# Two transformer blocks on one core: 32-block turns on VectorE, every row of V on TensorE, scores on 128 rows

## The reference

```python
# layer 0, first network: gated delta rule, 16 heads, both directions, chunk by chunk
a = eye + where(strict, kk * decay * beta[:, None], 0)
sol = triangular_solve(a, rhs, lower=True, unit_diagonal=True)
...
S = S * exp(g_last) + (k * exp(g_last - g)).T @ v_new
# after the mixer of both layers: 8 heads, 16 of 16384 experts per head and token
act = gelu(einsum('pd,phkd->phk', x, u_tab[idx]))
out = einsum('phk,phkd->pd', gate * act, v_tab[idx])
# layer 1: attention, 8 query heads and 2 key heads, keys normed by head, rope on the latent ones
# second network, layer 0: 8 heads of 64, causal, with a decay of its own per head
s = q @ k.T * scale + c_q[:, None] - c_k[None, :]
# second network, after each feed-forward part
x = x + sigmoid(rms_norm(x) @ w_gate) * (p @ w_proj)
```

## Time and profile before

| | |
|---|---|
| three timed runs | 4899.77 us median (4894.84 to 4905.21) |
| the profiled execution's own time | 4927.06 us |
| its span in the profile | 4925.3 us |
| PE / DVE / POOL / ACT busy | 80% / 55% / 45% / 19% |
| mean granted clock of PE | 0.894 |

### The profile page before, as it was taken

How to read it: one execution, slowest core, us unless ns; L and a number is a source line. 1 busy time by engine, 2 the same in 40 slices (tenths; PEclk the granted TensorE clock), 3 DMA queues, 4 the chain that set the end, 5 groups by cost and what they waited for, 6 DMA issues and landing times.

```text
span 4925.3 us, 42426 instructions
## 1 busy us (share of the span) xinstructions
PE 3919.4 (80%) x14663; PEld 2246.6 (46%) x14663; DVE 2713.6 (55%) x5536; ACT 931.8 (19%) x2167; POOL 2220.1 (45%) x1993
## 2 busy tenths in 40 slices
PE   6799999999967886776777778666667798875898
PEld 1459874598643332222222234433222356632584
DVE  1355653557446766666666634676665245729241
ACT  0234321333211211111111112111111111010100
POOL 1014420244117778777777750478777400008000
PEclk7699999999988988999888988888799879986899
DMA  9310002100149999999999971799999614330343
GB/s 372 113 52 1 1 27 77 43 1 1 43 159 360 380 349 347 375 379 368 394 383 372 387 273 52 257 380 361 355 373 375 248 63 129 124 117 1 105 152 122
DMA packets 380100, 1043.21 MB, mean 212 GB/s; under 512 B 31682, under 2 KB 115884, under 8 KB 379888
## 3 DMA queue, kind: packets, MB, share of 16 engines
q0 software_dynamic: 225424, 816.31, 44.3%
q1 hardware_dynamic: 154464, 224.18, 13.5%
HBM read 1039.29 MB, written 1.08 MB: 211 GB/s over the span
## 4 chain that ended last, share of the span: by engine, by line
PE 48%; POOL 15%; DMA 15%; DVE 12%; issue 7%; ACT 2%; DVEq 0%; POOLq 0%; ACTq 0%; SPq 0%
PE psum L261 12%; DMA arena<-in_peer_u,arena 9%; PE psum L1523 9%; POOL arena L1630 7%; POOL arena L1620 6%; DMA arena<-in_peer_v,arena 4%; PE psum L299 4%; PE psum L212 3%; PE psum L1041 3%; PE psum L717 3%; PE psum L1031 3%; PE psum L756 2%; DMA arena<-in_ada_w 2%; DVE arena L1690 2%; PE psum L1480 1%
## 5 line engine op out<-in xcount | busy, mean ns | idle before, releaser
L1523 PE MATMUL psum<-arena 128*128 128x512 f32 x2816 | 1438.8, 657 | 633.8 <-ACT arena L1562 335.7
L1690 DVE SCALAR_TENSOR_TENSOR arena<-arena 128x1024 bf16<-128x1024 f32 x768 | 938.9, 1225 | 704.5 <-DMA arena<-in_peer_u,arena 703.5
L1523 PEld LDWEIGHTS psum<-arena 128*128 128x128 f32 x2816 | 557.9, 209 | 1478.5 <-issue 1033.7
L1630 POOL DMA_INDIRECT arena<-in_peer_v,arena x768 | 886.9, 1155 | 248.1 <-issue 168.3
L1620 POOL DMA_INDIRECT arena<-in_peer_u,arena x768 | 848.5, 1105 | 298.8 <-issue 192.4
L261 PE MATMUL psum<-ring,arena 128*128 128x512 f32 (+2 forms) x1408 | 597.0, 588 | 27.2 <-DVE arena L2556 9.1
L261 PEld LDWEIGHTS psum<-ring,arena 128*128 128x128 f32 x1408 | 270.9, 200 | 349.1 <-issue 325.5
L212 PE MATMUL psum<-consts,arena 128*128 128x128 f32 (+1 forms) x1473 | 223.2, 300 | 171.1 <-DVE arena L362 84.5
L1140 POOL TENSOR_TENSOR arena<-arena 128x512 f32<-128x512 f32 x224 | 254.0, 1158 | 191.9 <-PE psum L1031 129.6
L299 PE MATMUL psum<-arena,ring 128*128 128x256 f32 x1408 | 312.7, 384 | 9.1 <-DVE arena L2551 7.7
L212 PEld LDWEIGHTS psum<-consts,arena 128*128 128x128 f32 (+1 forms) x1473 | 186.2, 155 | 237.4 <-issue 132.8
(11 more groups left out here) (380 smaller groups left out, 4042.0 us busy)
## 6 DMA issues: line engine op xcount, KB each, us to landing
arena<-in_ada_w SPq DMA_DIRECT2D x48, 1024.0 KB, 14.4
ring<-in_ffn_w_up SPq DMA_DIRECT2D x44, 1024.0 KB, 5.1
ring<-in_dn_w_in SPq DMA_DIRECT2D x24, 1024.0 KB, 5.3
ring<-in_peer_w_query SPq DMA_DIRECT2D x22, 1024.0 KB, 8.2
ring<-in_ffn_w_down SPq DMA_DIRECT2D x20, 1024.0 KB, 5.1
arena<-in_peer_u,arena POOLq DMA_INDIRECT x768, 6.3
arena<-in_peer_v,arena POOLq DMA_INDIRECT x768, 6.3
ring<-in_ev_w_in SPq DMA_DIRECT2D x10, 1024.0 KB, 5.2
```

Source lines behind the costliest of these rows:

```text
L1523: m = e.matmul(k.banks[4 + t % 2 * 2 + nh], self.diag[self.place[g] % self.ND], self.vsl[g % self.NV][:, nh * 512:(nh + 1) * 512], start=u ...
L1630: e.indirect_dma_start(self.vsl[g % self.NV], None, self.tables()[1], bass.IndirectOffsetOnAxis(ap=self.eid[u % 6][:, s:s + 1], axis=0)).t ...
L1690: e.scalar_tensor_tensor(self.junk[g % 2], self.us[g % self.NU], 1.0, self.h[:, u // 8, :], MUL, MUL, accum_out=self.a[u % 2][:, s:s + 1]) ...
```

## The change

In the delta rule the level-0 mask goes into T's buffer, T0 is made there in place, and a DVE transpose of 32x32 blocks makes P0 from it. The same DVE instruction makes T from P at levels 1 to 4; PE and ACT do that at level 5 only. In `Peer` the accumulator and the DVE's own slots are gone, and PE adds all 16 slots. In attention the four key tiles are normed and roped before q's transposes are awaited, with buffers of their own, and ACT takes their roots as each key tile is copied. In the even mixer q is copied by POOL into two buffers of 128 rows in which the other head's 64 rows are zero, and the decay's 8 rows stand in 128 with zeros. In `Ple` the load of p is issued by the stage before, and p is transposed and projected before the norm.

```diff
@@ delta rule, pe_chain
-                e.wait_ge(*G.at(key("lev0", ch)))
-                e.wait_ge(*V.at(key("Dk", ch)))
-                for h in range(4):
-                    m = self.turn(e, b0[:, h * 128:(h + 1) * 128], self.bufs[ch][0][:, h, :])
-                m.then_inc(*P.up(key("lev0", ch)))
...
-                    if l > 1:
-                        e.wait_ge(*S.at(key(f"T{l - 1}", ch)))
+                    if l == 6:
+                        e.wait_ge(*S.at(key("T5", ch)))
...
+                    if l < 6:
+                        e.wait_ge(*V.at(key(f"T{l - 1}", ch)))
...
-                if l < 6:
+                if l == 5:
@@ delta rule, pool_chain
-                    gL, D = self.bufs[ch][0], self.bufs[ch][1]
+                    gL, D = self.bufs[ch][3 if l == 0 else 0], self.bufs[ch][1]
@@ delta rule, dve_chain
+    def dve_turn(self, e, ch, src, dst):
+
+        a, b = (self.bufs[ch][n].rearrange("p h n -> p (h n)") for n in (src, dst))
+        return e.transpose(b, a)
...
-                e.tensor_tensor(T, rep(ident), gL, SUB).then_inc(*V.up(key("T0", ch)))
-                e.wait_ge(*P.at(key("lev0", ch)))
-                e.tensor_tensor(Pm, rep(ident), v4(self.two(ch)[0]), SUB).then_inc(*V.up(key("P0", ch)))
+                e.tensor_tensor(T, rep(ident), T, SUB).then_inc(*V.up(key("T0", ch)))
+                e.wait_ge(*V.now())
+                self.dve_turn(e, ch, 3, 4).then_inc(*V.up(key("P0", ch)))
...
                     e.tensor_tensor(Pm, Pm, v4(self.two(ch)[1]), SUB).then_inc(*V.up(key(f"P{l}", ch)))
+                    if l < 5:
+                        e.wait_ge(*V.now())
+                        self.dve_turn(e, ch, 4, 3).then_inc(*V.up(key(f"T{l}", ch)))
@@ Peer
-    OWN = (2, 6, 10, 14)
...
-            e.wait_ge(*(self.V.at(("own", old)) if self.own(old) else self.P.at(("y", old))))
+            e.wait_ge(*self.P.at(("y", g - self.NV)))
...
-                if s and u and self.own(16 * (u - 1) + s - 1):
-                    self.dve_own(e, u - 1, s - 1)
@@ attention, dve
+        for t in range(4):
+            x = self.kk[:, t, :].rearrange("p (h d) -> p h d", h=2)
+            e.wait_ge(*S.at(("k", t)))
+            e.wait_ge(*V.now())
+            norm_rows(e, V, S, x, 2, 128, self.gk.unsqueeze(1).to_broadcast([128, 2, 128]),
+                      self.sq[:, 0:256].rearrange("p (h d) -> p h d", h=2), self.stk[:, 2 * t:2 * t + 2], ("k", t))
...
         self.qt.dve(e)
@@ even mixer
+        for n in range(2):
+            e.memset(self.qz[n], 0.0).then_inc(*self.G.up())
+        e.memset(self.cz, 0.0).then_inc(*self.G.up("zero"))
+        e.memset(self.sel, 0.0).then_inc(*self.G.up())
...
+        for n in range(2):
+            rows = slice(64 * n, 64 * n + 64)
+            e.tensor_copy(self.qz[n][rows], self.qT[rows]).then_inc(*self.G.up("qz"))
...
-            e.matmul(b[:, 0:nk], self.qT[r0:r0 + 64, h // 2, t * 128:(t + 1) * 128], self.kT[r0:r0 + 64, h // 2, 0:nk],
-                     start=True, stop=False)
-            e.matmul(b[:, 0:nk], self.sel[0:8, h, :], self.cT[0:8, 0:nk], start=False, stop=True).then_inc(*P.up(("s", n)))
+            e.matmul(b[:, 0:nk], self.qz[h % 2][:, h // 2, t * 128:(t + 1) * 128], self.kT[:, h // 2, 0:nk], start=True, stop=False)
+            e.matmul(b[:, 0:nk], self.sel[:, h, :], self.cz[:, 0:nk], start=False, stop=True).then_inc(*P.up(("s", n)))
@@ Ple, pe
+        e.wait_ge(*self.lt.at("p"))
+        for t in range(2):
+            for c in range(2):
+                m = self.turn(e, self.k.banks[4][:, (2 * c + t) * 128:(2 * c + t + 1) * 128], self.p[:, t, c * 128:(c + 1) * 128])
+        m.then_inc(*self.P.up("pt"))
+        e.wait_ge(*self.V.at("pT"))
+        self.pp.pe(e)
         self.norm.pe(e)
...
-        self.pp.pe(e)
         self.gp.pe(e)
```

More of the change, by code:

```diff
@@ L1103, in act_chain @@
                     e.activation(self.bufs[ch][5], b0, ACT.Copy, bias=0.0, scale=1.0).then_inc(*S.up(key(f"X{l}", ch)))
-                if l < 6:
+                if l == 5:
                     for ch in self.chains:
                         b0 = self.two(ch)[0].rearrange("p (h n) -> p h n", h=4)
-                        e.wait_ge(*P.at(key(f"T{l}", ch)))
-                        e.activation(self.bufs[ch][3], b0, ACT.Copy, bias=0.0, scale=1.0).then_inc(*S.up(key(f"T{l}", ch)))
+                        e.wait_ge(*P.at(key("T5", ch)))
+                        e.activation(self.bufs[ch][3], b0, ACT.Copy, bias=0.0, scale=1.0).then_inc(*S.up(key("T5", ch)))
             for ch in self.chains:
@@ L1131, in pool_chain @@
                 for ch in self.chains:
-                    gL, D = self.bufs[ch][0], self.bufs[ch][1]
+                    gL, D = self.bufs[ch][3 if l == 0 else 0], self.bufs[ch][1]
                     if l == 0:
                         e.wait_ge(*V.at(key("Dk", ch)))
-                    elif l == 1:
-                        e.wait_ge(*P.at(key("lev0", ch)))
-                        e.wait_ge(*V.at(key("T0", ch)))
-                    else:
+                    elif l > 1:
                         e.wait_ge(*P.at(key(f"X{l - 1}", ch)))
@@ L1392, in __init__ @@
         self.l_v = [k.lane(f"v{n}_{name}_landed") for n in range(self.NV)]
-        self.pe_slots = [g for g in range(16 * self.units) if not self.own(g)]
-        self.place = {g: n for n, g in enumerate(self.pe_slots)}
-    def own(self, g):
-        return g < 128 and g % 16 in self.OWN
     def sc_mark(self, u):
@@ L1518, in pe_sum @@
             g = 16 * u + s
-            if not self.own(g):
-                e.wait_ge(*S.at(("dg", g)))
-                e.wait_ge(*self.l_v[g % self.NV].at(g))
-                for nh in range(2):
-                    m = e.matmul(k.banks[4 + t % 2 * 2 + nh], self.diag[self.place[g] % self.ND],
-                                 self.vsl[g % self.NV][:, nh * 512:(nh + 1) * 512], start=u % 8 == 0 and s == 0,
-                                 stop=u % 8 == 7 and s == 15)
-                m.then_inc(*P.up(("y", g)))
+            e.wait_ge(*S.at(("dg", g)))
+            e.wait_ge(*self.l_v[g % self.NV].at(g))
+            for nh in range(2):
+                m = e.matmul(k.banks[4 + t % 2 * 2 + nh], self.diag[g % self.ND], self.vsl[g % self.NV][:, nh * 512:(nh + 1) * 512],
+                             start=u % 8 == 0 and s == 0, stop=u % 8 == 7 and s == 15)
+            m.then_inc(*P.up(("y", g)))
             if s in steps:
@@ L1557, in act @@
                 g = 16 * u + s
-                if not self.own(g):
-                    n = self.place[g]
-                    if n >= self.ND:
-                        e.wait_ge(*P.at(("y", self.pe_slots[n - self.ND])))
-                    e.activation(self.diag[n % self.ND], k.const("ident"), ACT.Copy, bias=0.0,
-                                 scale=self.cf[u % 2][:, s:s + 1]).then_inc(*S.up(("dg", g)))
+                if g >= self.ND:
+                    e.wait_ge(*P.at(("y", g - self.ND)))
+                e.activation(self.diag[g % self.ND], k.const("ident"), ACT.Copy, bias=0.0,
+                             scale=self.cf[u % 2][:, s:s + 1]).then_inc(*S.up(("dg", g)))
                 if s - 3 in steps:
@@ L1669, in dve @@
         self.dve_add(e, self.nt - 1)
-    def dve_own(self, e, u, s):
-        V, g = self.V, 16 * u + s
-        c, v = self.cf[u % 2][:, s:s + 1], self.vsl[g % self.NV]
-        e.wait_ge(*self.l_v[g % self.NV].at(g))
-        e.wait_ge(*V.at(("cf", u)))
-        if u == 0 and s == self.OWN[0]:
-            e.tensor_scalar(self.acc, v, c, None, MUL).then_inc(*V.up(("own", g)))
-        else:
-            e.wait_ge(*V.at("own"))
-            e.scalar_tensor_tensor(self.acc, v, c, self.acc, MUL, ADD).then_inc(*V.up(("own", g)))
-        V.mark("own")
     def dve_dot(self, e, u, s):
@@ L1880, in __init__ @@
         self.gq, self.gk, self.cs = k.al(128), k.al(128), k.al(256)
-        self.st = k.al(8)
+        self.st, self.stk = k.al(8), k.al(8)
         self.sq = k.al(1024)
         self.tmp = [k.al(512) for _ in range(4)]
-        self.rots = [k.al(1024) for _ in range(2)]
+        self.rots, self.krots = [k.al(1024) for _ in range(2)], [k.al(256) for _ in range(2)]
         self.qT, self.kT = k.al2(8, 256), k.al2(2, 512)
@@ L1891, in __init__ @@
                                     for t in range(2)])
-        self.kt = [Turn(self, f"kT{t}", [(self.kk[:, t, :] if t < 2 else self.rots[t - 2][:, 0:256],
+        self.kt = [Turn(self, f"kT{t}", [(self.kk[:, t, :] if t < 2 else self.krots[t - 2],
                                          self.kT[:, :, t * 128:(t + 1) * 128], [lambda t=t: V.at(("k", t))])],
@@ L1959, in act @@
             e.activation(self.v[:, t, :], b[:, 256:512], ACT.Copy, bias=0.0, scale=1.0).then_inc(*S.up(("v", t)))
+            root_rows(e, self.V, S, self.stk[:, 2 * t:2 * t + 2], ("k", t))
         self.qt.act(e)
-        for t in range(4):
-            root_rows(e, self.V, S, self.st[:, 0:2], ("k", t))
         self.at.act(e)
@@ L2078, in __init__ @@
```

(7 more changed lines are left out.)

58 lines of the change are left out of this document (21 added, 37 removed).

## The result

The changed kernel takes 4759.57 us (median of 4 runs, 4734.30 to 4777.75) beside 4901.16 for the kernel before (4894.84 to 4905.21): a ratio of 0.9722, 95% interval 0.9698 to 0.9746, or 142 us. The forecast was 119 us less, and 4781. The profiled execution took 4734.30 us, the fastest of its four and 25 us under their median, where the profile of before was 26 us over the median of its four.

What follows compares the result with a forecast made beforehand. Stages run one after another, each with its own bound: PE's chain in the delta rule, neither PE nor DVE full in peer. Terms -48 - 39 - 12 - 16 - 4 = -119, from 4899.8 to 4781 us; range 4745 to 4868.

Steps and rivals of the forecast that it cites:

- A: Delta rule: DVE transposes of 0.70 us relieve PE's chain, which stays the bound narrowly; -48 us.
- step-through: Delta rule half followed by each engine's order, with waits for POOL: 345.0 us before, 320.7 after.
- signs of being wrong: DVE busy without rest in the levels, transposes of two lengths, or POOL waiting for PE; no size given.
- B: Peer stages: DVE's 32 operations a stage go to PE and POOL's issues shorten; `peer_a` -15, `peer_m` -24, together -39 us.
- C: Attention: key norms and ropes move into DVE's idle time, scores at about 3024; -12 us, -10 to -14.
- D: Even scores: matmuls on 128 rows are shorter and the clock may go to 1.00; -16 us, -7 to -22.
- fallback of -7 at half clock: Even scores: if the clock stays at half, only shorter matmuls gain, -7 us, 4790; chance inside the forecast's 0.60.
- E: Both Ple: 6.9 us leave L261's chain, but the norm's transposes come 5.0 later; -4 us, +4 to -10.
- Slow transposes: Delta rule rival: a DVE transpose takes 1.225 us and DVE bounds the level; +37 us there, 4866; chance 0.12.
- transposes that wait for POOL: Delta rule rival: DVE transposes wait for POOL as L1213 does; +31 us there, 4860; chance 0.12.
- PE as the bound of the peer stages: Rival: PE bounds both first tiles, waits behind L1480 eat gains; -12 us for the peer stages, 4808; chance 0.09.
- Half clock to the end of the even scores: Even scores rival: the clock stays at half, -7 us there, 4790; chance inside the forecast's 0.60.

Runs made afterwards that it cites:

- e4_turn_twice: Changed kernel with each DVE transpose of levels 1 to 4 made twice; 4936.65 us on another chip, delta stage 1275.4 us against 1190.1.
- e7_rhs_late: Changed kernel with three chains' right-hand side made after level 5 and the last's after level 4; ratio 0.9781 to the kernel before, 4830.2 us.
- e11: Changed kernel with the even scores' q and k product on 64 rows again, the decay's still on 128; even mixer 183.4 us against 167.5.
- e12: Changed kernel with the even scores' decay product on 8 rows again, q and k on 128; even mixer 185.6 us against 167.5.
- e5: The changed kernel itself once more, on the second chip, against the kernel before; ratio 0.9805, 93 us between the medians.
- e9: Changed kernel plus an unread two-SBUF-input DVE operation at each of 32 places per peer stage's first tile; 4816.78 us, ratio 0.9812 to the kernel before.
- e10: Changed kernel plus an unread one-input DVE sum over 128x1024 at each of the same 32 places per peer stage; 4777.19 us, ratio 0.9745 to the kernel before.
- e1: The kernel before with the delta rule's edits only; ratio 0.9908 to the kernel before on the same chip, -46 us.
- e8: Changed kernel with eight V buffers, late right-hand side, and Ple's norm transposes behind half of p's projection; 4815.02 us, ratio 0.9753 to the kernel before.

## Why the prediction was right, point by point

**A, the delta rule: -48 forecast, -51.6.** The transpose was taken as 0.70 us from the nearest one-input row and takes 0.712. What went otherwise is the sentence that PE stays the bound, narrowly. DVE was worked out as 6.6 us a level with both right-hand operations at 0.69; they take 1.1 to 1.5 each, and in the three later steps of a half the level is DVE's, 7.9 to 8.3 us. The step-through had the wait for POOL in it, and so the total was right where the sentence was not; `e4_turn_twice` shows DVE as the bound, and `e7_rhs_late` that these operations are the cause, 13.2 us where the step-through gave 12. Two of the forecast's own signs of being wrong showed: DVE busy without rest in the levels, and POOL waiting for PE. The later steps came out at 81 to 84 us against 87 to 90, inside the 80 to 86 that was said, the first at 76 against 84. The right total rests on the step-through, and that one is borne out.

The Trainium skill (SBUF — State Buffer, § Who interferes with whom) has two SBUF inputs as one condition under which a DVE instruction contends with a GpSimd instruction that reads SBUF. The trace agrees: 1227 ns for L1234 against 690, and 711 to 715 for every transpose.

**B, the peer stages: -39 forecast, -51 in the first comparison.** `peer_a` came as worked out (-15, measured -16), but by luck, from two larger terms that cancel: issues shorter by 39 us, not 21, and waits for PE of 23 us (256 x 0.09), not 6. The 21 was the issues under L1680 alone, and they are 20.7 us in the table above; nearly all of the rest are the issues under dot products, 19 us less (43.5 to 24.3), which the working put at nothing. The waits were put low beside a slip in PE's price: 27.7 us a stage is 64 records of 0.433, but a stage has 32 more slots of 4 records, 55 us, which leaves PE some 25 of its 81 idle us (the trace has 33). `peer_m`'s term was mis-sized: -24, measured -35. Its own two paces had given 31; the sum of overlaps, 20.6, pulled the choice down, for the same reason. What the forecast didn't see at all is that the pace differs from chip to chip: where an untouched unit takes 46 us the term is 8. The DMA share of 0.97 to 1.00 in the earlier trace rows was a hint of how little room the transfers leave.

**C: -12, measured -12.9.** The scores start 8.7 us after the last projection's end (2908.98 to 2917.73), where it was 21.2 (3015.02 to 3036.26). The third key tile was late too, not only the last, at no cost to the sum.

**D: -16, measured -18.6.** The choice to let the clock follow the rows of the matmuls held, and `e11` and `e12` show it. The fallback of -7 at half clock wasn't tested: with half of the edit the other matmul keeps its old length, and the two kernels gained 2.7 and 0.5 us, about what the untouched stage varies by. Its price per matmul was right: 0.47 us taken, 0.43 measured on 128 columns.

**E: -4, measured -6.8.** 6.9 us left L261's chain and the norm's transposes came late; in the second `Ple` L261's remaining part began 2.7 us later after the stage's start, not 5.0, as the transposes ran at full clock right behind p's projection. In the first one 2.6 us were gained in all.

**The rivals.** Slow transposes and transposes that wait for POOL are excluded by 711 to 715 ns. PE as the bound of the peer stages holds as a wait of 23 us in `peer_a`, not as more. Half clock to the end of the even scores is excluded; the first 8 us were at half. And the forecast was met with some luck of the chip: the same change was worth 142 us here and 93 on the chip of `e5`, with 119 between them.

## What to carry to other kernels

When an engine takes over work, cost it together with what its other operations will meet at their new times: here the transposes themselves were cheap, and the two right-hand operations per level, moved under GpSimd's work, made DVE the bound and cost 13 us until they were put elsewhere. The same goes for what an engine gives up: taking 32 operations off DVE took 21 us off the issues under them in `peer_a` and another 19 off those under its other work. An edit to a stage that lives on its transfers was worth 51 us on one chip and 8 on another, so measure such edits on more than one. And compare stages that an edit doesn't touch before two profiles are subtracted.

## What the runs showed of the hardware

- A DVE transpose of 32x32 blocks in float32 on 128x512 took 711 to 715 ns in all 160 cases, whether GpSimd's work overlapped it (122) or not (38); a DVE operation with two inputs in SBUF on the same shape (L1234) took 1074 to 1472 ns there and 0.69 us undisturbed.
- An issue of an indirect DMA on GpSimd took 0.94 us. Where it began under a DVE operation with two inputs in SBUF on 128x1024, it ended 0.81 to 0.82 us after that operation's end: 64 issues of 1.58 us in the mean in `e9`, against 63 of 0.945 under a reduction of the same length in `e10`. A one-input `tensor_scalar` on 128x1024 held two issues in the same way (1.149 us).
- The granted clock stayed at 0.50 over 40 us (3869.6 to 3910 in `e11`) in which PE was busy without rest and half of its score matmuls used 64 rows, and likewise with 8 rows in `e12`; with all on 128 rows it was 1.00 from 12 us after the scores' start.
- At half clock, two score matmuls on 128 columns that follow each other start 0.43 us apart if both use 128 rows, and 0.72 apart if they use 64 and 8.
- Peer units that no edit touches took 42.2 to 45.7 us in the first comparison and on the chip of `e9` to `e12`, and 45.5 to 47.1 on those of `e1` to `e4` and `e5` to `e8` (means of 7 or 8 units); why is open.
